# First expert layer: the shared expert's four token tiles moved from the end of the job list to its head, with their results stored and read back

## What is computed

```python
def moe_ffn(h, w_router, e_bias, w_gate, w_up, w_down, s_gate, s_up, s_down):
    scores = jax.nn.sigmoid((h @ w_router).astype(jnp.float32))
    _, idx = lax.top_k(scores + e_bias.astype(jnp.float32), TOP_K)      # TOP_K = 8 of 64
    wts = jnp.take_along_axis(scores, idx, axis=-1)
    wts = wts / wts.sum(-1, keepdims=True) * ROUTE_SCALE
    ...
    def expert_block(args):
        tok, e = args
        xb = h_pad[tok]
        a = jax.nn.silu(xb @ w_gate[e]) * (xb @ w_up[e])
        return a @ w_down[e]
    ...
    shared = (jax.nn.silu(h @ s_gate) * (h @ s_up)) @ s_down
    return routed + shared
```

## Time and profile before

| | us |
|---|---|
| median of 3 runs | 3094.17 (3092.8 to 3102.18) |
| the profiled execution, its own time | 3094.74 |
| its span | 3092.9 |
| TensorE busy in the span | 2708.4 (88%) |
| VectorE, ScalarE, GpSimd busy | 1208.7, 857.4, 184.7 |
| moved by DMA | 778.74 MB, mean 252 GB/s |
| first load of expert weights of this layer issued | 360.03 |
| first and last expert product on TensorE start | 395.51, 982.09 |
| next stage's first gather of result rows | 996.50 |

### The profile page before, as it was taken

How to read it: one execution, slowest core, us unless ns; L and a number is a source line. 1 busy time by engine, 2 the same in 40 slices (tenths; PEclk the granted TensorE clock), 3 DMA queues, 4 the chain that set the end, 5 groups by cost and what they waited for, 6 DMA issues and landing times. The chain is left out here.

```text
span 3092.9 us, 45075 instructions
## 1 busy us (share of the span) xinstructions
PE 2708.4 (88%) x18056; PEld 1905.5 (62%) x18056; DVE 1208.7 (39%) x1954; ACT 857.4 (28%) x1256; POOL 184.7 (6%) x152
## 2 busy tenths in 40 slices
PE   5887599899997599699988959989889989898798
PEld 4666444343342287454544439978559979797698
DVE  2443642211111735422222145459544454445443
ACT  1142111111112123111111124326434353334442
POOL 0000300122000410000000000000100000000000
PEclk8998699999998799899999979999989989999899
DMA  8823699999997643379999965333335345241541
GB/s 327 317 113 136 280 380 426 410 392 366 426 389 295 273 137 157 122 331 425 409 425 424 425 251 223 149 115 137 123 150 204 153 187 203 93 174 49 223 181 75
DMA packets 111757, 778.74 MB, mean 252 GB/s; under 512 B 28089, under 2 KB 29689, under 8 KB 59225
## 3 DMA queue, kind: packets, MB, share of 16 engines
q1 hardware_dynamic: 90472, 717.79, 57.8%
q0 software_dynamic: 12432, 35.75, 3.0%
q10 hardware_dynamic: 8672, 22.71, 1.9%
HBM read 739.41 MB, written 42.61 MB: 253 GB/s over the span
## 5 line engine op out<-in xcount | busy, mean ns | idle before, releaser
L3177 PE MATMUL psum<-second_x_hi,ffn_up_hi 128*128 128x256 f32 x1408 | 403.0, 286 | 22.1 <-DVE ffn_up_lo L3286 22.1
L3177 PE MATMUL psum<-second_x_lo,ffn_up_hi 128*128 128x256 f32 x1408 | 402.2, 286 | 0.0
L3177 PE MATMUL psum<-second_x_hi,ffn_up_lo 128*128 128x256 f32 x1408 | 402.0, 286 | 0.0
L3177 PEld LDWEIGHTS psum<-second_x_hi,ffn_up_hi 128*128 128x128 f32 x1408 | 274.2, 195 | 24.9 <-DVE ffn_up_lo L3286 23.5
L3177 PEld LDWEIGHTS psum<-second_x_lo,ffn_up_hi 128*128 128x128 f32 x1408 | 274.4, 195 | 1.4
L3177 PEld LDWEIGHTS psum<-second_x_hi,ffn_up_lo 128*128 128x128 f32 x1408 | 274.0, 195 | 0.0
L1585 PE MATMUL psum<-experts_ahead_ring_up,moe_cols 128*64 128x512 f32 x1056 | 235.1, 598 | 0.0
L3254 DVE TENSOR_TENSOR ffn_up_lo<-second_ring_up,ffn_up_hi 128x4096 fp32r<-128x4096 f32 x40 | 177.0, 4425 | 109.9 <-ACT ffn_up_hi L3214 109.9
L1585 PEld LDWEIGHTS psum<-experts_ahead_ring_up,moe_cols 128*64 128x64 f32 x1056 | 73.2, 137 | 138.3 <-issue 137.6
L1949 DVE TENSOR_TENSOR experts_gated<-experts_silu,psum 128x256 f32<-128x256 f32 (+1 forms) x57 | 21.3, 374 | 326.6 <-ACT experts_silu L1735 326.6
L3214 ACT ACTIVATE ffn_up_hi<-second_ring_up 128x4096 fp32r<-128x4096 f32 x40 | 144.5, 3612 | 1.2 <-DMA second_ring_up<-in_ffn 1.2
(11 more groups left out here) (639 smaller groups left out, 5107.4 us busy)
## 6 DMA issues: line engine op xcount, KB each, us to landing
experts_ahead_ring_up<-in_experts SPq DMA_DIRECT2D x65, 2048.0 KB
moe_ring_up<-in_experts SPq DMA_DIRECT2D x65, 2048.0 KB
second_ring_up<-in_ffn SPq DMA_DIRECT2D x44, 2048.0 KB, 9.2
experts_ahead_ring_down<-in_experts SPq DMA_DIRECT2D x65, 1024.0 KB
moe_ring_down<-in_experts SPq DMA_DIRECT2D x65, 1024.0 KB
second_ring_down<-in_ffn SPq DMA_DIRECT2D x44, 1024.0 KB
second_ring_up<-in_attn_w_qkv SPq DMA_DIRECT2D x9, 2048.0 KB
results<-experts_y ACTq DMA_DIRECT2D x33, 512.0 KB
```

Of the source, the lines that this page charges most:

```text
L3177: last = nc.tensor.matmul(psum[:, 2 * m + kind, 0:LAT], w[:, j, k, at], h[:, k, :], start=k == 0 and which == 0, stop=k == KD - 1 and whic ...
```

## The change

Four parts go together.

1. `ORDERS[0]` puts the four shared jobs first. They are jobs 0 to 3 now and the shared weights are item 0, loaded first; the order of the pairs is as it was. A shared job takes its columns straight from the columns of `h` that the stage before left in `cols`, which are token tile by token tile where units 0 to 3 have their place, so it gathers and turns nothing. The first real units are number 4 and up.
2. The 12 list rounds are spread: one before the gates of job 0, then four (three in job 0) behind the copied gates of jobs 0, 1 and 2. The list product stands in job 3, behind the up product of job 4. The later routing steps move by four jobs.
3. The kept loads are five up items and four down items (shared and first four experts), in turn, instead of four and four.
4. The routing's scratch tiles fill `acc` while the shared jobs run, so their results cannot go there. They are stored like those of full jobs, to 512 new rows of `results` (2 MB), and SP reads them into `acc` behind its last weight load, once VectorE has finished with the scratch tiles (job 26).

```diff
@@ -40,10 +40,10 @@
...
-ORDERS = ((0, 1, 6, 7, 17, 8, 9, 18, 10, 11, 19, 12, 13, 20, 2, 3, 21, 4, 5, 22, 14, 15, 23, 16, 24, 25, SHARED, SHARED, 26, SHARED, SHARED, *range(27, 32)),
+ORDERS = ((*[SHARED] * 4, 0, 1, 6, 7, 17, 8, 9, 18, 10, 11, 19, 12, 13, 20, 2, 3, 21, 4, 5, 22, 14, 15, 23, 16, *range(24, 32)),
...
-LIST_B_JOB, ROWS_JOB, OWNERS_JOB, SHARES_JOB, TABLE_UNIT = 9, 10, 16, 18, 16
+LIST_A_JOB, LIST_B_JOB, ROWS_JOB, OWNERS_JOB, SHARES_JOB, TABLE_UNIT = 3, 13, 14, 20, 22, 20
@@ -1152,8 +1152,9 @@
...
-        self.early = 0
-        while all(r is not None and r[0] < KEPT for r in self.regions[self.early]):
+        self.n_shared, self.early = tokens // P, 0
+        at = next(u for u in range(self.units) if self.regions[u][0] is not None)
+        while all(r is not None and r[0] < KEPT for r in self.regions[at + self.early]):
@@ -1259,10 +1260,9 @@
...
-        for pair in range(KEPT // 2):
-            for item in (2 * pair, 2 * pair + 1):
-                self.load_up(sp, item, self.place(item))
-            for item in (2 * pair, 2 * pair + 1):
+        for item in range(KEPT + 1):
+            self.load_up(sp, item, self.place(item))
+            if item < self.down_depth:
@@ -1304,11 +1304,12 @@
...
-    turns_for = {j: u for u, j in enumerate(first_job)}
-    fulls = [sum(job[0] == "full" for job in jobs[0:j]) for j in range(n_jobs + 1)]
+    n_shared = plan.n_shared
+    assert all(job[0] == "shared" and job[2] == t for t, job in enumerate(jobs[0:n_shared]))
+    turns_for = {first_job[u]: u for u in range(n_shared, n_units)}
...
-    n_fulls, n_smalls = fulls[n_jobs], smalls[n_jobs]
+    n_wides, n_smalls = wides[n_jobs], smalls[n_jobs]
@@ -1330,7 +1331,7 @@
...
-    loads = [(when_up(item), "up", item) for item in range(KEPT, n_items)] + [(when_down(item), "down", item) for item in range(KEPT, n_items)]
+    loads = [(when_up(item), "up", item) for item in range(KEPT + 1, n_items)] + [(when_down(item), "down", item) for item in range(ring.down_depth, n_items)]
@@ -1393,7 +1394,8 @@
...
-        tables_loaded = st.sem("tables_loaded")
+        tables_loaded, scratch_free, shared_back = st.sem("tables_loaded"), st.sem("scratch_free"), st.sem("shared_back")
+        shared_at = plan.result_units * P + spare * SPARE
@@ -1443,6 +1445,12 @@
...
+            sp.wait_ge(scratch_free, 1)
+            for f in range(2):
+                sp.wait_ge(stored[f], 16 * (n_shared // 2))
+            for t in range(n_shared):
+                sp.dma_start(acc[:, t, :], results[shared_at + t * P:shared_at + (t + 1) * P, :]).then_inc(shared_back, 16)
+            sp.wait_ge(shared_back, 16 * n_shared)
@@ -1464,15 +1472,13 @@
...
-                if q >= 2:
-                    pool.wait_ge(turned, q - 1)
-                if jobs[first_job[q]][0] == "shared":
-                    t = plan.tile_of[q]
-                    nc.gpsimd.dma_start(x_rows[:, q % 2, :], h_dram[t * P:(t + 1) * P, :]).then_inc(gathers[q % 2], 16)
-                    return
-                if q < n_early:
-                    pool.wait_ge(early_known, 1 if q == 0 else 2)
-                    table = who_early
+                n = q - n_shared
+                if n >= 2:
+                    pool.wait_ge(turned, n - 1)
+                at = q
+                if n < n_early:
+                    pool.wait_ge(early_known, 1 if n == 0 else 2)
+                    table, at = who_early, n
@@ -1480,7 +1486,7 @@
...
-                                             in_offset=bass.IndirectOffsetOnAxis(ap=table[:, q:q + 1], axis=0),
+                                             in_offset=bass.IndirectOffsetOnAxis(ap=table[:, at:at + 1], axis=0),
@@ -1492,7 +1498,7 @@
...
-            for q in range(n_units):
+            for q in range(n_shared, n_units):
@@ -1623,17 +1629,19 @@
...
-                    pe.wait_ge(gathers[q % 2], 16 * (q // 2 + 1))
-                    if q >= 1:
...
-                        pe.wait_ge(turned_out, 2 * q)
+                    n = q - n_shared
+                    pe.wait_ge(gathers[q % 2], 16 * (n // 2 + 1))
+                    if n >= 1:
...
+                        pe.wait_ge(turned_out, 2 * n)
...
-                pe.wait_ge(turned_out, 2 * unit + 2)
+                if kind != "shared":
+                    pe.wait_ge(turned_out, 2 * (unit - n_shared) + 2)
@@ -1658,8 +1666,6 @@
...
-            pe.wait_ge(lists_ready, 1)
-            list_units(LIST_A, LISTED).then_inc(listed_out, 1)
@@ -1667,7 +1673,7 @@
...
-                if j == 0:
+                if j == LIST_A_JOB + 1:
@@ -1676,6 +1682,10 @@
...
+                if j == LIST_A_JOB:
+                    pe.wait_ge(gates_out, j + 1)
+                    pe.wait_ge(lists_ready, 1)
+                    list_units(LIST_A, LISTED).then_inc(listed_out, 1)
@@ -1721,10 +1731,9 @@
...
-                    act.wait_ge(turned, q + 1)
-                    if q >= 4:
...
-                        act.wait_ge(ups, last_job[q - 4] + 1)
+                    act.wait_ge(turned, q - n_shared + 1)
...
+                    act.wait_ge(ups, last_job[q - 4] + 1)
@@ -1860,11 +1867,14 @@
...
-            for r in range(rounds_a):
-                list_round(r)
-                if r == 1:
-                    dve.wait_ge(by_expert_ready, 1)
-                    then(v.tensor_copy(by_expert.rearrange("p s e -> p (s e)"), psum[:, 0, 0:5 * n]))
...
+            def first_rounds(j):
...
+                for r in range(max(1, rounds_a * j // LIST_A_JOB), rounds_a * (j + 1) // LIST_A_JOB):
+                    list_round(r)
+                    if r == 1:
+                        dve.wait_ge(by_expert_ready, 1)
+                        then(v.tensor_copy(by_expert.rearrange("p s e -> p (s e)"), psum[:, 0, 0:5 * n]))
@@ -1923,8 +1933,8 @@
...
-                if two_lists and 1 <= j <= rounds_b - rounds_a:
-                    list_round(rounds_a + j - 1)
+                if two_lists and LIST_A_JOB < j <= LIST_A_JOB + rounds_b - rounds_a:
+                    list_round(rounds_a + j - LIST_A_JOB - 1)
@@ -1948,8 +1958,7 @@
...
-            dve.wait_ge(listed_out, 1)
-            v.tensor_scalar(who[:], psum[:, GATE_T, LIST_A:LIST_A + n_units], -1.0, float(tokens), ALU.mult, ALU.add).then_inc(who_ready, 1)
+            list_round(0)
@@ -1958,6 +1967,11 @@
...
+                if j < LIST_A_JOB:
+                    first_rounds(j)
+                if j == LIST_A_JOB:
+                    dve.wait_ge(listed_out, 1)
+                    v.tensor_scalar(who[:], psum[:, GATE_T, LIST_A:LIST_A + n_units], -1.0, float(tokens), ALU.mult, ALU.add).then_inc(who_ready, 1)
@@ -1967,13 +1981,13 @@
...
-                if jobs[j][0] == "full":
-                    f = fulls[j]
+                if j == SHARES_JOB + tok_tiles:
+                    v.memset(spent[:, 0:1], 0.0).then_inc(scratch_free, 1)
+                if jobs[j][0] != "third":
+                    f = wides[j]
...
-                elif jobs[j][0] == "shared":
-                    v.tensor_copy(acc[:, plan.tile_of[unit_of(j)], BANK:D], psum[:, DOWN + 1, :]).then_inc(y_high, 1)
@@ -3424,7 +3438,7 @@
...
-                idle = results[PLANS[0].result_units * P:, :]
+                idle = results[PLANS[0].result_units * P:PLANS[0].result_units * P + PLANS[0].spare * SPARE, :]
@@ -4202,7 +4216,7 @@
...
-        results = nc.dram_tensor("results", [PLANS[0].result_units * P + PLANS[0].spare * SPARE, D], F32, kind="Internal").ap()
+        results = nc.dram_tensor("results", [PLANS[0].result_units * P + PLANS[0].spare * SPARE + TOK, D], F32, kind="Internal").ap()
```

22 lines of the change are left out of this document (10 added, 12 removed).

## The result

| | before | after |
|---|---|---|
| median | 3096.61 us (3092.8 to 3102.18, 6 runs) | 3111.28 us (3107.89 to 3113.38, 6 runs) |
| ratio to before | | 1.0041, 95% interval 1.0032 to 1.0051 |
| the profiled execution, its own time | 3094.74 | 3108.99 |
| its span | 3092.9 | 3107.2 |
| first load of this layer's expert weights issued | 360.03 | 361.01 |

The change makes the kernel 14.7 us slower by the medians and 14.3 by the profiled executions. (The ratio is not that of the two medians: 1.0041 would make it 12.7 us, the interval 9.9 to 15.8.) The forecast was 3110, slower by 15. Of the difference 13.8 us are there when the next stage gathers its first result rows, and 1.0 of these was there before the first weight load. So 12.8 of the 14.3 us belong to this stage.

A forecast was written before the change was run, and what follows sets the result against it. Weight transfers were taken to bound the stage up to 838 us, TensorE after. Real jobs 34.6 us later and a transfer-bound end put the last product at 1000.7 against 985.7: 3094.7 + 15 = 3110 us, range 3097 to 3121.

The forecast's parts named there:

- its cold price: First shared up product on TensorE: extra time because the clock is partly at its lower level, 2 us (1.2 to 6.9).
- second real up product later by: Start of the layer: second up product of a real expert starts at 439.9 instead of 405.3, 34.6 us later (32 to 41).
- DMA near nothing: Start of the layer, 410 to 440 us: weight loads wait for full slots, losing some 12 MB of transfers.
- stalls at: TensorE's two long waits before a down product, at 547 and 838 us, come back 34.6 us later.
- the two large terms: Head: real jobs start 34.6 us later. End: 45.8 us of TensorE work goes, but transfers then outlast TensorE.
- No gain, since the ring was full either way: Weight slots at the start: items 5 and 6 loaded instead of 4 and 5, so the later stalls do not shrink.
- rival 2: Transfers use part of the idle start, or middle stalls shrink: 9 of the 15 us won, +6, 3101; chance 0.14.
- The tail's transfer time: Stretch behind the second long stall: remaining transfers take 117 us by rate, 129 by counted tiles; 121 taken.
- Rival 1: TensorE stays the bound to the stage's end: -45.8 + 34.6 = -11 us, 3083.5; chance 0.08.
- Rival 3: More is lost: first product all cold (+5), end by the tile count (+7): +22 to +27, 3119; chance 0.12.
- Rival 4: First shared product waits for the routing instead of starting beside it; adds to rival 3, chance included there.
- The rule weighed in the prediction: Interleaving stretches with different bounds helps: shared jobs cost least between weight-hungry pairs, removing them leaves only loading; sum +15 us.

The follow-up runs named there:

- the series of one to four jobs: The changed kernel with one, two, three or all four shared jobs first, the others near the end: +1.0, +8.9, +14.4, +20.7 us over the kernel before.
- no_shared: The kernel before with its four shared jobs left out: 3481.22 us in total, not comparable; tail 129.05 us, 18.6 saved.
- the second comparison: The changed kernel run again beside the kernel before on another chip: 20.7 us slower, ratio interval 1.0048 to 1.0084.
- before_itself: The kernel before, unchanged, run against itself on another chip: 3096.29 us, ratio 1.0002.
- before_half_down: The kernel before with the down weights of experts from rank 48 on loaded by half (8.4 MB fewer): 3092.57 us, ratio 0.9997.
- after_again: The changed kernel itself, run again on the chip of the one-to-four-jobs kernels: 20.7 us over before, ratio interval 1.0048 to 1.0084.
- after_half_down: The changed kernel with the down weights of experts from rank 48 on loaded by half (8.4 MB fewer): 3098.06 us, ratio 1.0009.
- one_first: The changed kernel with one shared job first and three near the end, shared weights loaded twice: ratio 0.9997 to before; repeated, 3092.81 us, 0.9996.

## Why the prediction was right, point by point

| step, as the prediction put it | forecast | measured |
|---|---|---|
| first shared up product starts at | 384.3 | 385.37, less 1.0 that was late before the stage |
| its cold price | 2 (1.2 to 6.9) | 1.74 (8.77 - 7.03) |
| from its end to the turned gates | 1.0 | 1.00 |
| second real up product later by | 34.6 (32 to 41) | 35.5, less 1.0 |
| DMA near nothing in 410 to 440 | "near nothing" | 119 GB/s in 410 to 430, 134 in 404 to 444 |
| transfers that the idle time loses | 12 MB | 9.1 MB (404 to 444) |
| stalls at | 582 and 872.7 | 580.69 and 872.54, less 1.0 |
| last pair's up product starts | 983.9 (993.7 - 9.8) | 982.84, less 1.0 |
| from there to the end | 16.9 (17.9 - 1) | 17.0 |
| tail without shared jobs | 128 (1000.7 - 872.7) | 127.3 |
| wait per pair at the end | 4 to 6 | 2.4 to 5.6, in five pairs |
| last product ends at | 1000.7 | 999.85, less 1.0 |
| read-back and stores | 0, at most 2 | 0 |
| next stage's gather later by | 15 | 13.8, less 1.0 |
| time | 3110 | 3111.28, 14.7 more than before |

Each of the two large terms was right by itself, and the sum is not right by chance: the head's by the timeline and by the series of one to four jobs, the end's by its two parts in the table and by `no_shared` (18.6 saved, where 19.6 follow from the forecast's 128). 34.5 us of delay at the long stall, 1.0 of it from before the stage, and 20.3 of shortening leave 14.1 at the last product. The stage's own 12.8 us at the gather are 2.2 fewer than forecast: 1.1 at the long stall, 0.7 in the tail, 0.3 behind it. That 14.7 by the medians comes nearer to 15 than this is luck, as the 20.7 of the second comparison says too.

What was less good:
- "No gain, since the ring was full either way" was argued from the queue alone. The second real up product was 35.5 us later, the product behind the long stall 34.5, and the stalls were 6.05 and 6.57 us before, 4.06 and 5.79 after. So some 1 us of the idle start was won back (rival 2), if that much: the same kernel's stalls differ by more between profiles (4.27 and 2.55 in `before_itself`).
- "DMA near nothing" left out what else runs in that time: the four shared stores (2.1 MB), three gathers, and the up load that takes the shared item's place at 425 (2.1 MB). Only 410 to 425 is near nothing, with 62 GB/s. The bytes lost were 9 MB and not 12. It changed no term, because the loss was carried in the delay of the jobs and not counted from the bytes.
- The tail's transfer time was chosen between 117 and 129. Up to 1000 the profile moved 416 GB/s x 127 us = 52.8 MB, of which 2.1 are the rows read back, so 50.7 MB; the forecast had 49.9, the count by tiles 54.8 (its own tiles add up to 54.5). The measured row was the better guide.
- Rival 1, TensorE bound to the end, fell on both counts that it named: TensorE is busy 107.08 of 127 us, and the windows of the new tail show 427 GB/s and not 490.
- Rival 3 (7 to 12 us more) did not come. After four of five waits the product was cold, but the transfers were the bound beside them, so that a cold product should cost nothing until the last pair, which was counted. That last step is argued; no run tries it.
- Rival 4 fell with the first row of the head.

The rule weighed in the prediction (Trainium skill, "Perfetto Trace Analysis", Optimization Strategy), that performance may be improved by interleaving stretches with different bounds, is borne out by the series here, and the series adds where the limit lies: of the four jobs, the first to leave the end was worth 9.6 us of its 11.45, the next two 1.5 together, since they were filling time that the weights needed anyway.

## What to carry to other kernels

Work that needs no bytes is a filler, and a filler belongs where the stream is the bound and the buffers are not yet full. Put ahead of a ring of fixed depth it is hidden only while TensorE would wait anyway and the ring still has room (here the first job of the four, which delayed the others by 2.5 us); past that, each microsecond of it delays all that follows and in the end stops the stream. Before moving work out of a stretch in which one engine is 100% busy, divide the bytes that remain there by the best rate that any window shows: where that time is the longer one, it is what is left (117 to 129 us here, where TensorE alone would need 102). A busy share of 1.00 on TensorE in the idle window, and of 0.84 in the new tail, told the wrong story in both places; the DMA share beside it told the right one.

## What the runs showed of the hardware

- **The weight rate differs between profiles of the same kernel, and a stage that is paced by weights shows it.** The stretch 440 to 830 of the kernel before, in the first profile and in `before_itself`:

```profile
440.00:830.00 390.00, 380.21 (x2799) 154.64 (x2799) 81.16 (x208) 59.86 (x123) 63.25 (x64) 0.99 0.99 404
```

```profile
440.00:830.00 390.00, 383.64 (x2827) 157.19 (x2819) 81.66 (x210) 60.22 (x124) 63.45 (x64) 0.99 0.99 407
```

  404 against 407 GB/s. That is 0.7% of 390 us, some 3 of the 6 us by which the second stall and the gather stand earlier (832.12 and 990.68 against 838.08 and 996.50); the rest stays open. On two chips the kernels that differ from before only at the end of the stage moved 407 and 408 GB/s (`no_shared`, `before_half_down`, `before_itself`); which chip gave the 404 is not known, and with one profile of each it isn't shown that the chip is the cause. Absolute times from two profiles are not to be compared to a few microseconds; the tails (147.7, 147.8) may be.
- **The change's cost was 14.7 us in one comparison and 20.7 in another** (intervals 1.0032 to 1.0051 and 1.0048 to 1.0084, which overlap in their ends). By the gather it is 13.8 in the first pair of profiles and 17.4 between `before_itself` and `after_again`, which come from two chips; counted from the first weight load, 12.8 and 15.0. What of that is the chip and what is chance stays open.
- **A product behind a short wait is cold or not at nearly the same idle time.** In the kernel after, an up product took 8.78 us behind 2.79 and behind 3.11 us of idle, 8.41 behind 5.55, and 7.09 behind 2.41; in `after_half_down` 8.78 behind 2.39. In the second expert layer an up product took 5.35 us behind 1.86 of idle and 3.66 behind 1.75. Idle time alone does not tell. Nor does the start of work tell when the clock comes back: at 2289.24 and 2289.36 in two kernels of which one had begun 3.3 us earlier, and one block before 3.4 us apart, like their starts.
- **The profiled execution can be the fastest of its kernel**, as it is in three of these kernels: 3088.04 of 3088.04 to 3102.1 in `one_first`, 3088.23 of 3088.23 to 3099.83 in `before_itself`, 3107.86 of 3107.86 to 3119.58 in `after_again`. In `before_itself` its mean granted clock is 0.937, that of the three slowest runs 0.932 to 0.934. A sum that starts from a profiled execution is of use for differences, and may sit up to 8 us under a median.
